# The dense V product of an expert layer: weights stationary instead of moving

## The reference, cut to what matters

```
x = x + peer_ffn(rms_norm(x), ...)          # T = 256 tokens, D = 1024
...                                         # idx, g: 128 picks and weights of each token
ue, ve = u[ib], v[ib]                       # rows of u and v, 16384 x 1024 each
act = jax.nn.gelu(jnp.einsum('pd,phkd->phk', hb, ue))
return jnp.einsum('phk,phkd->pd', gb * act, ve)
```

## Time and profile before

| what | us |
|---|---|
| median of 3 runs (lowest, highest) | 2423.35 (2417.65, 2425.61) |
| the profiled execution's own time | 2420.36 |
| its span, first to last instruction | 2418.6 |
| TensorE matmuls busy | 2311.1 (96%) |
| VectorE busy | 1775.4 (73%) |
| ScalarE busy | 1418.6 (59%) |
| DMA, mean over the span | 214 GB/s |

### The profile page before, as it was taken

The page is one execution under the profiler, slowest core; times in us unless marked ns, Lnnn a source line. Parts: engine busy times, 40 slices in busy tenths (PEclk is TensorE's granted clock), DMA queues, the critical chain, the costliest instruction groups (busy, mean ns, idle before and its releaser), DMA issues.

```text
span 2418.6 us, 50834 instructions
## 1 busy us (share of the span) xinstructions
PE 2311.1 (96%) x16182; PEld 2114.4 (87%) x16186; DVE 1775.4 (73%) x4072; ACT 1418.6 (59%) x3234; POOL 659.7 (27%) x545
## 2 busy tenths in 40 slices
PE   8998998999999899999999989889999989999998
PEld 8998887999999778888899978889999988788887
DVE  4667775578876688888856667755788857888887
ACT  5576654555655555555555777555556556555554
POOL 0000200007777622222100011000087776222220
PEclk9999999999999999999999999999999999999999
DMA  6565645457777679989745556454577775889895
GB/s 219 186 201 182 224 136 173 157 190 193 191 199 185 162 257 317 313 300 322 238 159 165 196 188 205 149 170 158 186 195 195 193 179 152 295 308 316 307 322 187
DMA packets 191038, 518.16 MB, mean 214 GB/s; under 512 B 56988, under 2 KB 67412, under 8 KB 190676
## 3 DMA queue, kind: packets, MB, share of 16 engines
q1 hardware_dynamic: 122484, 413.64, 49.7%
q0 software_dynamic: 64512, 100.82, 17.3%
q10 hardware_dynamic: 3936, 2.46, 0.4%
HBM read 497.73 MB, written 21.66 MB: 215 GB/s over the span
## 4 chain that ended last, share of the span: by engine, by line
PE 84%; DVE 7%; ACT 5%; issue 2%; DMA 1%; ACTq 1%; DVEq 0%; POOL 0%; SPq 0%; POOLq 0%
PE bank L321 16%; PE bank L322 16%; PE bank L323 16%; PE bank L336 9%; PE bank L338 9%; PE bank L337 9%; DVE w_lo L303 3%; ACT w_hi L290 2%; PE bank L1744 1%; ACT L363 1%; DVE hot L1683 1%; PE bank L1100 1%; ACT hot L1410 1%; PE bank L1720 1%; PE bank L417 1%
## 5 line engine op out<-in xcount | busy, mean ns | idle before, releaser
L303 DVE TENSOR_TENSOR w_lo<-raw,w_hi 128x512 fp32r<-128x512 f32 x1512 | 1020.3, 688 | 551.0 <-ACT w_hi L290 538.7
L290 ACT ACTIVATE w_hi<-raw 128x512 fp32r<-128x512 f32 x1512 | 906.6, 627 | 394.3 <-PE bank L338 319.0
L321 PE MATMUL bank<-h_hi,w_hi 128*128 128x224 f32 (+1 forms) x3360 | 949.5, 283 | 26.3 <-DVE w_lo L303 25.9
L322 PE MATMUL bank<-h_lo,w_hi 128*128 128x224 f32 (+1 forms) x3360 | 937.4, 279 | 0.0
L323 PE MATMUL bank<-h_hi,w_lo 128*128 128x224 f32 (+1 forms) x3360 | 937.0, 279 | 0.0
L321 PEld LDWEIGHTS bank<-h_hi,w_hi 128*128 128x128 f32 x3360 | 649.8, 193 | 39.2 <-DVE w_lo L303 31.3
L322 PEld LDWEIGHTS bank<-h_lo,w_hi 128*128 128x128 f32 x3360 | 650.2, 194 | 1.0 <-issue 0.5
L323 PEld LDWEIGHTS bank<-h_hi,w_lo 128*128 128x128 f32 x3360 | 650.0, 193 | 0.0
L1254 POOL DMA_INDIRECT spread_w<-mass,cell_at x256 | 437.6, 1709 | 444.2 <-DVE mass L1568 302.1
L336 PE MATMUL bank<-w_hi,a_hi 128*128 128x512 f32 x1088 | 425.7, 391 | 12.8 <-DVE a_lo L435 7.9
L338 PE MATMUL bank<-w_hi,a_lo 128*128 128x512 f32 x1088 | 423.5, 389 | 0.0
(11 more groups left out here) (220 smaller groups left out, 2276.0 us busy)
## 6 DMA issues: line engine op xcount, KB each, us to landing
raw<-stream SPq DMA_DIRECT2D x756, 512.0 KB
spread_w<-zeros POOLq DMA_DIRECT2D x32, 512.0 KB, 3.7
h_hi<-spread_w POOLq DMA_DIRECT2D x32, 512.0 KB, 5.7
hank<-rel_hankel SPq DMA_DIRECT2D x16, 256.0 KB, 2.7
spread_w<-mass,cell_at POOLq DMA_INDIRECT x256
rel_hankel<-rel_line SPq DMA_DIRECT2D x16, 192.0 KB
hank<-rel_hankel SPq DMA_DIRECT2D x16, 128.0 KB, 2.1
A<-subkeys SPq DMA_DIRECT2D x2, 1024.0 KB, 6.3
```

The lines of the kernel that those rows point to most:

```text
L290: act.activation(w_hi[:, (ring % 2) * 2 + k, :], raw[:, slot, sub, 512 * k:512 * k + 512], ACT.Copy).then_inc(w_hi_done, 1)
L303: dve.tensor_tensor(w_lo[:, q, :], raw[:, slot, sub, 512 * k:512 * k + 512], w_hi[:, q, :].bitcast(F32), ALU.subtract).then_inc(w_parts, 1)
L321: pe.matmul(ps, hi, rhs_hi(4 * k + c), start=first, stop=False)
L322: pe.matmul(ps, hi, rhs_lo(4 * k + c), start=False, stop=False)
```

## The change

The V loop's roles are exchanged. Pieces of 128 x 128 of the weights are the stationary operand. `a_hi` and `a_lo` become two parts of one tile `a_two`, so that one matmul moves both, 2 x 224 = 448 columns, for the high weights, and a second moves the 224 of the high part for the low weights. Eight pieces of a block go to eight banks; in each bank the high part's and the low part's sums lie side by side (448 of 512 columns), with features on the partitions and tokens along the columns.

At the end ScalarE copies one half of each bank to `y` (in `A`'s space), VectorE adds the other half, and TensorE turns `y` back with 16 full-precision matmuls against the identity, into four banks whose tokens are on the partitions; VectorE adds these to `x`. The own tokens' matmuls now come after the last block, into banks that the turned tiles then add to. `y`'s 32 own columns are zeroed in V's block 100; the zeroing of `a_hi` and `a_lo` goes. The squares' scratch tile moves.

The eight lane copies and the load of `square` move from ScalarE's queue to SP's, between the loads of pairs 64 and 65 (blocks 113 and 114 of U).

```diff
+        a_two = sb(top, "a_two", [P, 2, 2, SEQ], F32R)
+        a_hi, a_lo = a_two[:, :, 0, :], a_two[:, :, 1, :]
...
+        def up_values(pe, b, ring, k_blk, first, last=False):
+            blk, a = b + place.first, ring % 2
+            pe.wait_ge(a_parts.sem, k_blk + (a_parts.base + 1))
+            for k in range(2):
+                q = a * 2 + k
+                pe.wait_ge(w_parts, blk * 2 + (k + 9))
+                for c in range(4):
+                    acc = bank[4 * k + c]
+                    both = acc[:, 0:2 * N_DENSE].rearrange("p (i n) -> p i n", i=2)
+                    hi, lo = w_hi[:, q, P * c:P * c + P], w_lo[:, q, P * c:P * c + P]
+                    if last:
+                        pe.matmul(acc[:, 0:N_DENSE], lo, a_two[:, a, 0, N_OWN:SEQ], start=False, stop=False)
+                        pe.matmul(both, hi, a_two[:, a, :, N_OWN:SEQ], start=False, stop=True).then_inc(v_acc.sem, 1)
+                    else:
+                        pe.matmul(both, hi, a_two[:, a, :, N_OWN:SEQ], start=first, stop=False)
+                        ins = pe.matmul(acc[:, 0:N_DENSE], lo, a_two[:, a, 0, N_OWN:SEQ], start=False, stop=False)
+                if not last:
+                    ins.then_inc(w_used, 1)
...
@@ peer_sync @@
+                def own_lanes():
+                    sp.wait_ge(feat_done.sem, feat_done.base + 1)
+                    for g in range(LANE_GROUPS):
+                        for i, kept in enumerate((own_at, picks[:, 2, :])):
+                            sp.dma_start(lane[N_OWN * g:N_OWN * g + N_OWN, i, :], kept[0:N_OWN, OWN_PICKS * g:OWN_PICKS * g + OWN_PICKS]).then_inc(lanes_in.sem, 16)
+                    sp.dma_start(square[:], cst[:, C_SQUARE:C_REP]).then_inc(feat_in.sem, 16)
+                load_pairs(sp, 2, 65)
+                own_lanes()
                 if layer + 1 < DEPTH:
-                    load_pairs(sp, 2, PEER_BLOCKS // 2 + 2)
+                    load_pairs(sp, 65, PEER_BLOCKS // 2 + 2)
...
@@ peer_scalar @@
                 act.wait_ge(feat_done.sem, feat_done.base + 1)
-                for g in range(LANE_GROUPS):
-                    for i, kept in enumerate((own_at, picks[:, 2, :])):
-                        act.dma_start(lane[...], kept[...]).then_inc(lanes_in.sem, 16)
-                act.dma_start(square[:], cst[:, C_SQUARE:C_REP]).then_inc(feat_in.sem, 16)
                 act.dma_start(feat_dram[layer], feats[:]).then_inc(feat_out.sem, 16)
...
+                for c in range(DC):
+                    act.wait_ge(v_acc.sem, v_acc.base + c + 1)
+                    act.activation(y[:, c, N_OWN:SEQ], bank[c][:, 0:N_DENSE], ACT.Copy).then_inc(y_half.sem, 1)
@@ peer_vector @@
-                dve.memset(a_hi[:, :, 0:N_OWN].bitcast(F32), 0.0)
-                dve.memset(a_lo[:, :, 0:N_OWN].bitcast(F32), 0.0)
...
+                    if k == 100:
+                        dve.memset(y[:, :, 0:N_OWN], 0.0)
...
-                add_to_x(dve, bank[4:8])
+                for c in range(DC):
+                    dve.wait_ge(y_half.sem, y_half.base + c + 1)
+                    dve.tensor_tensor(y[:, c, N_OWN:SEQ], y[:, c, N_OWN:SEQ], bank[c][:, N_DENSE:2 * N_DENSE], ALU.add).then_inc(y_done.sem, 1)
+                for t in range(TT):
+                    for k in range(2):
+                        part = x[:, t, 512 * k:512 * k + 512]
+                        dve.wait_ge(y_turned.sem, y_turned.base + 2 * k + t + 1)
+                        dve.tensor_tensor(part, part, bank[2 * k + t][:, :], ALU.add).then_inc(x_done.sem, 1)
@@ peer_tensor @@
-                down_block(pe, B_V, 0, 0, bank[4:8], True, PEER_COLS)
-                blocks_loop(pe, B_V + 1, N_V - 2, lambda k, blk, ring, n, i: down_block(pe, blk, ring, k + 1, bank[4:8], False, PEER_COLS))
+                up_values(pe, B_V, 0, 0, True)
+                blocks_loop(pe, B_V + 1, N_V - 2, lambda k, blk, ring, n, i: up_values(pe, blk, ring, k + 1, False))
+                up_values(pe, PEER_BLOCKS - 1, (PEER_BLOCKS - 1) % 4, N_V - 1, False, True)
                 pe.wait_ge(row_used.sem, row_used.base + 2 * OWN_PICKS)
                 for k in range(2):
-                    pe.matmul(bank[6 + k][:, :], turn_own, own[:, 512 * k:512 * k + 512], start=False, stop=False)
-                down_last(pe, PEER_BLOCKS - 1, (PEER_BLOCKS - 1) % 4, N_V - 1, bank[4:8], PEER_COLS)
+                    pe.wait_ge(y_done.sem, y_done.base + 2 * k + 2)
+                    pe.matmul(bank[2 * k + 1][:, :], turn_own, own[:, 512 * k:512 * k + 512], start=True, stop=False)
+                for k in range(2):
+                    pe.wait_ge(y_done.sem, y_done.base + 4 * k + 4)
+                    for t in range(TT):
+                        for c in range(4):
+                            ins = pe.matmul(bank[2 * k + t][:, P * c:P * c + P], y[:, 4 * k + c, PEER_COLS[t]], ident, start=t == 0, stop=t == 0 or c == 3)
+                        ins.then_inc(y_turned.sem, 1)
+                pe.sem_inc(w_used, 2)
```

More of the change, by code:

```diff
@@ L193, in trunk @@
         h_lo = sb(top, "h_lo", [P, DC, SEQ], F32R)
-        a_hi = sb(top, "a_hi", [P, 2, SEQ], F32R)
-        a_lo = sb(top, "a_lo", [P, 2, SEQ], F32R)
+        a_two = sb(top, "a_two", [P, 2, 2, SEQ], F32R)
+        a_hi, a_lo = a_two[:, :, 0, :], a_two[:, :, 1, :]
         ss = sb(top, "ss", [P, TT, 2])
@@ L220, in trunk @@
         h_hi_done, h_done = flag("h_hi_done", DC, DC), flag("h_done", DC, DC)
-        acc_done, x_done = flag("acc_done", 2 * TT, 2 * TT), flag("x_done", 2 * TT, 2 * TT)
+        acc_done, x_done = flag("acc_done", 2 * TT, 0), flag("x_done", 2 * TT, 2 * TT)
         small_in = flag("small_in", 4 * 16)
@@ L251, in trunk @@
         own_in = flag("own_in", 0, 16)
+        v_acc, y_half, y_done, y_turned = flag("v_acc", 0, DC), flag("y_half", 0, DC), flag("y_done", 0, DC), flag("y_turned", 0, 2 * TT)
         gain_row_in, rep_scaled, rep_mm, rep_done = flag("gain_row_in", 0, 16), flag("rep_scaled", 0, 1), flag("rep_mm", 0, 1), flag("rep_done", 0, 1)
@@ L1212, in trunk @@
             end_A = KEYS * N_DENSE
-            junk = whole_A[:, 0:8 * SEQ].rearrange("p (a b) -> p a b", b=SEQ)
+            y = whole_A[:, 0:8 * SEQ].rearrange("p (a b) -> p a b", b=SEQ)
+            junk = whole_A[:, 8 * SEQ:16 * SEQ].rearrange("p (a b) -> p a b", b=SEQ)
             keys_t = whole_A[:, end_A - 80 * P:end_A - 64 * P].rearrange("p (a k) -> p a k", k=KEYS)
@@ L1282, in peer_sync @@
                 sp.dma_start(row[:, 0, :], spread(ffn_g[layer:layer + 1], 0, P)).then_inc(gain_row_in.sem, 16)
+                def own_lanes():
[6 more added lines that the diff above has]
+                own_lanes()
                 if layer + 1 < DEPTH:
-                    load_pairs(sp, 2, PEER_BLOCKS // 2 + 2)
+                    load_pairs(sp, 65, PEER_BLOCKS // 2 + 2)
                 else:
-                    load_pairs(sp, 2, PEER_BLOCKS // 2 - 8)
+                    load_pairs(sp, 65, PEER_BLOCKS // 2 - 8)
                     sp.wait_ge(g_done.sem, g_done.base + N_GROUPS + 2)
@@ L1393, in peer_scalar @@
                 act.wait_ge(feat_done.sem, feat_done.base + 1)
-                for g in range(LANE_GROUPS):
-                    for i, kept in enumerate((own_at, picks[:, 2, :])):
-                        act.dma_start(lane[N_OWN * g:N_OWN * g + N_OWN, i, :], kept[0:N_OWN, OWN_PICKS * g:OWN_PICKS * g + OWN_PICKS]).then_inc(lanes_in.sem, 16)
-                act.dma_start(square[:], cst[:, C_SQUARE:C_REP]).then_inc(feat_in.sem, 16)
                 act.dma_start(feat_dram[layer], feats[:]).then_inc(feat_out.sem, 16)
```

## The result

The changed kernel takes 2367.5 us (median of 4 runs, 2366.6 to 2370.2) against 2423.2 us before: a ratio of 0.977, 95% interval 0.976 to 0.979. That is 56 us less, where 44 were forecast (2379 us, range 2357 to 2404). The profiled execution took 2367.7 us.

What follows compares the result with a forecast made beforehand. V was taken as bound by TensorE, with VectorE and the DMA close behind. Terms -56 + 4 + 14 - 15 + 2 + 8 = -43 us on 2420.4 gave 2377, predicted as a median of 2379 us, range 2357 to 2404.

Steps and rivals of the forecast that it cites:

- V's blocks: V loop: a block falls from 2.72 to 2.50 us, -56 us over 2 layers x 128 blocks.
- the DMA's term: V: weight loads get less time to land, 0.06 us a block on 118 blocks a layer, +14 us.
- VectorE's lumps: V: row sums followed by a spread product next block stop TensorE, 8 places, +4 us (0 to 8).
- The nine DMAs: U near block 118: issuing them from SP, not ScalarE, removes TensorE's stop and clock loss, -15 us.
- SP's queue: U near block 114: nine issues delay the next weight load, 1 us a layer, +2 us (0 to 8).
- The tail: End of V: own matmuls, 16 turns and last adds take 4 us more a layer, +8 us (+5 to +12).
- rival A: V runs free; VectorE's and the DMA's +18 us do not appear: 2361 us; chance 0.14.
- B: The DMA sets V's pace, blocks with rows take 2.64 us: 2398 us; chance 0.16.
- C: V: 448 columns cost as 512 or as two passes, 2.69 us a block: 2410 us; chance 0.08.
- D: U: the nine DMAs stall TensorE from SP as from ScalarE, 5 to 7 us a layer: 2392 us; chance 0.06.
- E: V: late loads stop TensorE until the granted clock falls, 7 us each; 2449 us at 10 events; chance 0.05.
- if the granted clock in V leaves 1.00: V: one of the signs named in advance as showing the prediction wrong; no size of its own.

Runs made afterwards that it cites:

- thin_fetch: The changed kernel with each row fetch of the own tokens cut to 64 of 1024 columns, VectorE's work unchanged in length: 2364.4 us.
- more_dma: The changed kernel with 30 more loads of 512 KB a layer during V, issued by GpSimd into an unused tile: 2371.2 us.
- sp_only: The kernel before with only the move of the nine DMAs from ScalarE's queue to SP's: 2407.6 us.
- spaced: The changed kernel with V's row sums moved so that none stands in the block before a spread product: 2360.2 us.
- more_dma_before: The kernel before with 60 extra loads of 512 KB beside V in all: 2428.2 us.
- best: spaced, with block 0 of V getting its spread product first and turned tiles made in the order of VectorE's adds: 2358.4 us.

## Why the prediction was right or wrong

**V's blocks: right.** 2.507 us measured, 2.50 forecast; the gain of the bare pace is 0.213 x 256 = 54.5 us for 56. The estimate of 448 from two measured sizes held for the pair and not for its two members; that their errors cancelled was luck.

**What V's faster blocks meet: the DMA's term failed.** "I take 0.06 us a block [...]: +14 us." It measures at most 3 us (`thin_fetch`), and about 0 in the row of splits 66 to 121; with 13% more traffic it is still nothing (`more_dma`). The step that misled was a margin of waiting at ScalarE, read as a loss at TensorE. ScalarE did come to wait for the stream, as forecast (22.8 us), but it had time to spare: for the most part it exchanged one wait for another (105.7 us for TensorE is left). The 6.0 us of landing rose to 7.4 and did no harm for the same reason. The share of 0.995, worked out "if packets keep their times", did not come either: it was 0.94, where 0.95 or more was named as a sign. From share, count and time of the DMA views a packet took 0.169 us on the mean in V before (900 to 1000) and 0.160 after (880 to 980).

**VectorE's lumps: right mechanism, too small.** Forecast +4 us for both layers, at four places a layer; range 0 to 8. Splits 66 to 121 lost 2.4 us a layer before (152.0 less 55 x 2.72) and 6.6 and 5.6 after (144.5 and 143.5 less 137.9): +7. One of the places, in the rows of TensorE and of its weight loader:

```profile
1022.16 0.47 PE L366 MATMUL bank<-a_two,w_hi 128*128 128x448 f32 x1 [0.89 <-DVE a_two L456]
...
1022.15 0.19 PEld L366 LDWEIGHTS bank<-a_two,w_hi 128*128 128x128 f32 x1 [1.16 <-DVE w_lo L304]
```

The loader's 5.0 us and the matmuls' 3.7 us are the same five stops, at the starts of blocks. By the starts of the matmuls the four stops cost 0.62, 0.40, 0.40 and 0.40 us before and 1.01 to 1.05 each after. That is 0.57 more each on the mean where "what two blocks get shorter" gave 0.44: +4.6 for both layers. The other 3 us are a fifth stop of 0.38 us in the first layer, and delays of some 0.1 us, which no row of waits lists: 22 and 15 of them among the row sums, where the kernel before has 4. The prediction's term has neither.

**The nine DMAs: right.** -15 forecast, -14.8 in the table, -14.2 as `sp_only` measures it. The +2 for SP's queue did not come: the blocks around 114 kept their pace.

**The tail: right.** +8 forecast, +7.0 measured. After the last block come the own matmuls and the turns:

```profile
1176.41 2.34 ACT L1472 ACTIVATE A<-bank 128x224 f32<-128x224 f32 x8
...
1177.15 2.47 DVE L1736 TENSOR_TENSOR A<-A,bank 128x224 f32<-128x224 f32 x8
...
1178.20 1.88 PE L1805 MATMUL bank<-hot,picks 128*128 128x512 f32 x4
...
1179.92 3.73 PE L1810 MATMUL bank<-consts,A 128*128 128x128 f32 x32
...
1181.01 0.69 DVE L1741 TENSOR_TENSOR x<-x,bank 128x512 f32<-128x512 f32 x1 [1.39 <-PE bank L1810]
...
1182.79 1.88 DVE L1741 TENSOR_TENSOR x<-x,bank 128x512 f32<-128x512 f32 x3 [1.10 <-PE bank L1810]
```

Copies and adds of `y` end at 1179.62, before the own matmuls do, as forecast; the 32 records of the turns take 3.73 us (3.7 forecast); VectorE then waits 1.10 us for a turned tile whose add is next in its order but third in TensorE's.

**The sum.** Without the DMA's 14 us and SP's 2, with 3 more for the lumps and 1 less for the tail, the forecast of -43 would have been -57; the profiles differ by 52.7, the medians by 55.6. So 2379 stands 11.5 us above the 2367.5 measured, near the lower end of its own range, and rival A (2361: VectorE's and the DMA's terms both absent) was nearer, too fast by about the lumps alone; `spaced` reaches it. Rivals B and C are refuted by `more_dma` and by the pair's 0.314 us, D by `sp_only`. E did not occur: inside V, with eight banks a block, the clock stays at 1.00. At V's very start the changed kernel has one stretch at the lower clock of 1.2 GHz a layer, 6.8 us long in the first (in the row 845 to 855 with its granted clock of 0.66) and 3.4 in the second, which the kernel before did not have there; taken by the letter, the sign "if the granted clock in V leaves 1.00" was there. `sp_only`, without V's change, has one in its second layer and `more_dma_before` in both; `spaced` has none in its first and `best` none at all. So it is not tied to the change by these runs. Ahead of it lies TensorE's stop of 2.8 us or more before V, which all but `best` share, with and without such a stretch. The splits 0 to 62 show its price: 2.2 and 0.9 us above 62 x 2.507, where `spaced` without it has 0.2.

## What to carry to other kernels

Roles of a matmul are worth exchanging when the smaller operand can move in both its parts under one load of weights: here 16 matmuls of 448 and 224 columns beat 12 of 512: 5376 columns move in place of 6144, 12.5% fewer, and a block takes 7.8% less time. A wait that appears on a helper engine is a loss only if the engine that sets the pace waits too; take the load away and look at that engine's row. Where a helper is 86 to 93% busy, as VectorE is here among the row sums, its order matters more than its sum: the same work spread one lump per two blocks was worth 7 us.

## What was not expected of the hardware

The DMA engines' busy share is no measure of the room left: 312 GB/s showed as 0.91, 345 as 0.94, and 391 GB/s still ran at 1.00 with TensorE busy all the time. The mean packet of that stretch took 0.149 us, against 0.160 at 341 GB/s and 0.169 at 312: the share is made of times that shrink as the traffic grows. A matmul of 224 columns cost 0.111 us in a stream of its kind and 0.102 behind one of 448; one of 448 cost 0.211. A moving operand in two pieces with a gap of 32 columns ran 1% faster than the same 448 columns in one piece (0.211 against 0.214 us), though its place in memory differed too. And the same program part, mixing and router of the second layer, took 450.6 to 456.8 us from kernel to kernel, with 6.8 to 20.5 us of it at the lower clock.
